# Rotary projection stage: other order of projections, scores one block ahead, sine product written by DVE in four pieces

## The chip, the cores and the metric

The kernel runs on one core of a Trainium2 chip. The metric is the device time of one execution in microseconds (us), the median of a few runs. Engines are named as in the profile: PE is TensorE's matmul, PEld its weight load, DVE is VectorE, ACT is ScalarE, POOL is GpSimd, SP is SyncE, which here issues most of the DMAs.

## The reference, cut to what matters

Sixteen meta tokens and 512 frames (L = 528 tokens of 1024 features) go through two layers. A layer has an attention and pooling half and a gated MLP half:

```
xn = rms_norm(h, attn_norm_g[l]);  q, k, v, u = split(xn @ w_in[l])      # 512, 128, 128, 512 columns
q = apply_rope(rms_norm(q, q_norm_g[l]), cos, sin) * HEAD_DIM ** -0.5     # 8 heads of 64
k = apply_rope(rms_norm(k, k_norm_g[l]), cos, sin)                        # 2 heads of 64
attn = sliding_sink_attention(q, k, v, sinks[l])    # chunks of 64, a window of 2 chunks, plus meta keys
pool = multiscale_pool(u, w_pool[l], pool_scale[l]) # 4 groups of 128 channels, trailing means over 2/4/8/16
h = h + concat(attn, pool) @ w_out[l]
xn = rms_norm(h, ffn_norm_g[l]);  h = h + (gelu(dwconv(xn @ w_gate)) * (xn @ w_up)) @ w_down
```

The rotation of a head is `[x1*c - x2*s, x2*c + x1*s]` with x1, x2 the two halves of 32 features: each half needs the other half's product with the sine.

## The kernel before

Features lie on the partitions and tokens on the free axis, so a tile is 128x528. Each fp32 operand is split into a high and a low part (`x_hi`, `x_lo`, `w_hi`, `w_lo`; line 443 makes three products of them), and ACT (line 337) and DVE (line 348) make the two parts of each weight unit of 256 columns, which SP loads into `raw`. One projection of 128 columns is 8 feature tiles x 3 products x 2 token halves, 48 matmuls.

Five engine programs are written out by hand and run in parallel, with semaphores between them; nothing reorders them. An engine does its instructions in the written order, so one that waits holds up everything behind it. PE's order in a layer's first half is: projections k, v, the column mean of the squares for the norm (L453), q0, the transposes of v (`v_T`, L513), the mean of k's squares, q1, q2, the q means of the first two heads' tiles (`q_means`, L499), q3, u3 and the first 5 of 48 rows of the remaining u groups, the second q means, and then the loop over the 9 blocks of queries: `scores` (L561), some rows of the side projection (`project_side`, u2, u1, u0, which go through a slice of PSUM called slot 4), `heads` (L588, L595), `probs_T` (L573, L576), and the four maps of the pooled groups.

The rotation of the four q tiles and of k works through DVE, ACT and POOL. DVE scales the projected tile (L1078, `head` or `k_dup`), multiplies it by the sine table into a buffer `sine`, which is the tile of v_T (L1097, for k L1094), ACT copies `sine` to `rot_s` with the 32-partition quarters swapped (`shift`, L844, four copies), POOL multiplies by the cosine (`rot_c`, L729, L724) and adds the two into `q_rot` (L733 for the meta tokens, L734 for the rest); k's sum is made by DVE in four pieces (L1131). There is one `rot_c`, one `rot_s` and one `sine`, so a tile's rotation waits for the one before.

```
def shift(n):
    act.wait_ge(sine_ready, l * 5 + (n + 1))
    ...
    for to, fr in ((0, 32), (32, 0), (64, 96), (96, 64)):
        ins = nc.scalar.activation(rot_s[to:to + 32], sine[fr:fr + 32], ACT.Copy)
    ins.then_inc(rots_ready, 1)
```

In the block loop, step b has PE's scores of block b, DVE's row maxima of b (L1170 to L1175), ACT's exponentials of b (L919), and DVE's division of block b-1 (L1181 to L1189).

Of the kernel before, what the change touches and what calls it, by code (L numbers as in the profile page):

```python
# [28 lines left out]
EPS = 1e-6  # L29
# [17 lines left out]
U_KV, U_Q, U_U23, U_U01, U_POOL, U_OUT = 0, 1, 3, 4, 5, 6  # L47
# [16 lines left out]
class Psum:  # L64
# [7 lines left out]
    def __init__(self):  # L72
        self.at, self.uses = {}, [0, 0, 0, 0, 0]
        order = [("k", 2), ("v", 3), ("attn_norm", 0), ("q0", 1), ("v_T", 0), ("k_sq", 3), ("q1", 2),
                 ("q2", 1), ("qn0", 0), ("q3", 3), ("u3", 2), ("qn1", 0)]
        for b in range(NB):
            order += [(f"scores{b}", 1 - b % 2)] + {5: [("pool3", 1)], 8: [("pool2", 0), ("pool1", 0)]}.get(b, [])
        order += [("pool0", 1)] + [(f"{kind}{b}", s) for b in range(NB) for kind, s in (("probs_T", 2), ("heads", 3))]
        order += [(f"u{g}{half}", 4) for g in (2, 1, 0) for half in "ab"]
# [21 lines left out]
def build_trunk(nc, x, meta_tokens, attn_norm_g, w_in, q_norm_g, k_norm_g, sinks, w_pool, pool_scale,  # L101
# [5 lines left out]
    with ExitStack() as ctx:  # L107
# [26 lines left out]
        eps = sb(ctx, "eps", [P, 1])  # L134


        with ExitStack() as sc:
# [18 lines left out]
            sine = v_T[:]  # L156
            rot_c = sb(sc, "rot_c", [P, L])
            rot_s = sb(sc, "rot_s", [P, L])
# [20 lines left out]
        with ExitStack() as sc:  # L179
            x_in = sb(sc, "x_in", [P, SEQ // P, D_MODEL])  # L180
            meta_in = sb(sc, "meta_in", [N_META, D_MODEL])
            par_in = sb(sc, "par_in", [NPAR, DEPTH, P])
            sink_in = sb(sc, "sink_in", [P, DEPTH, 2, 2])
            y_out = sb(sc, "y_out", [P, SEQ // P, D_MODEL])

# [7 lines left out]
        def tok(ap):  # L193
# [12 lines left out]
        eps_ready = sem("eps_ready")  # L206
        h_copied = sem("h_copied")
# [12 lines left out]
        sine_ready = sem("sine_ready")  # L220
        rots_ready = sem("rots_ready")
# [19 lines left out]
        MIX_ORDER = ["heads0", "heads1", "heads2", "pool3", "heads3", "heads4", "heads5", "pool2", "heads6",  # L241
                     "pool1", "heads7", "heads8", "pool0"]
# [11 lines left out]
        GROUPS = (3, 2, 1, 0)  # L254
# [3 lines left out]
        POOLED_AT, POOL_HI_AT, POOL_LO_AT, MAP_AT = (1, 4, 6, 9), (2, 5, 7, 9), (3, 6, 9, 9), (5, 8, 9, 10)  # L258
# [16 lines left out]
        def rotated_before(l, n):  # L275

            name = ROTATED[n - 1]
# [28 lines left out]
        def last_user_done(l, unit, i=0):  # L306
# [17 lines left out]
            else:  # L324
                name = ("v", "q1", "q3", "u2b", "u0b", "pool0")[old]
# [40 lines left out]
        def _(sp):  # L366
            sp.dma_start(cst[:, 0:C_CNT], const[:, 0:C_CNT]).then_inc(ident_loaded, 16)
            kv_cols = blocks(w_in[0])[:, :, ATTN_WIDTH:ATTN_WIDTH + UC]
            for t in range(SEQ // P):
                if t == 2:  # L370
                    sp.dma_start(raw[0][:, :, 0:P], kv_cols[:, :, 0:P]).then_inc(kraw_loaded, 16)
                sp.dma_start(x_in[:, t], x[0, t * P:(t + 1) * P, :]).then_inc(x_loaded[t], 16)
            for a in (0, 4):
                sp.dma_start(raw[0][:, a:a + 4, P:UC], kv_cols[:, a:a + 4, P:UC]).then_inc(raw_loaded[0], 16)
# [45 lines left out]
        def _(pe):  # L420
# [61 lines left out]

            eight = [(k, k) for k in range(KT)]
            for l in range(DEPTH):
                def project(name, unit, ready=None):
                    c = int(name in ("v", "u3", "q1", "q3"))
# [3 lines left out]
                    elif c == 0 or name == "u3" or (l == 0 and name == "v"):  # L490
# [868 lines left out]
```

## Time and profile before

| what | value |
|---|---|
| median of 3 runs | 1100.2 us (1099.22 to 1102.31) |
| the profiled execution, its own time | 1100.07 us |
| its span (first to last instruction) | 1098.3 us |
| PE busy | 1064.2 us, 97% of the span |
| DVE busy, ACT busy, POOL busy | 522.4, 471.3, 123.3 us |
| mean granted TensorE clock | 0.988 of full speed |

A busy share is a mean over stages. The MLP halves take most of the span and the attention halves lie at 17 to 127 us and at 561 to 667 us; what a change of the attention half is worth is read there, from what PE waits for.

### The profile page before, as it was taken

How to read it: one execution, taken by the hardware profiler on the slowest of the kernel's cores; microseconds unless marked ns; L12 is line 12 of the kernel's file. 1: busy time of each engine (PE TensorE's matmuls, PEld its weight loads, DVE VectorE, ACT ScalarE, POOL GpSimd, SP SyncE). 2: the span in 40 equal slices, each digit the busy share in tenths (PEclk: the TensorE clock that was granted, in tenths of full speed). 3: DMA queues.
4: the chain of work that ended last, by engine and by line, in shares of the span. 5: the costliest groups of instructions: out<-in, count | busy, mean ns of one | idle time of the engine just before them, and what ended most of it. 6: DMA issues, size and time to landing. Idle time of an engine off the chain costs nothing.

```text
span 1098.3 us, 18457 instructions
## 1 busy us (share of the span) xinstructions
PE 1064.2 (97%) x7668; PEld 1001.0 (91%) x7668; DVE 522.4 (48%) x690; ACT 471.3 (43%) x662; POOL 123.3 (11%) x121
## 2 busy tenths in 40 slices
PE   6998899999999999999999989999999999999997
PEld 6897799999999999999999978999988999888886
DVE  5667645545445545232336576455455544532221
ACT  5775435444444444122237664364344543421110
POOL 1262000111000111000003510000001100000000
PEclk9989999999999999999999899999999999999999
DMA  6311222322322322323321112223223232233212
GB/s 201 103 49 40 77 77 77 103 89 77 114 76 76 105 86 70 103 78 105 104 78 49 39 40 97 96 77 108 84 76 114 77 111 80 76 106 106 72 61 77
DMA packets 93518, 94.30 MB, mean 86 GB/s; under 512 B 3392, under 2 KB 91800, under 8 KB 93480
## 3 DMA queue, kind: packets, MB, share of 16 engines
q1 hardware_dynamic: 92768, 93.01, 26.4%
q0 software_dynamic: 400, 0.58, 0.2%
q8 instruction: 27, 0.44, 0.2%
q10 hardware_dynamic: 312, 0.18, 0.1%
q14 instruction: 11, 0.09, 0.0%
HBM read 91.65 MB, written 2.10 MB: 85 GB/s over the span
## 4 chain that ended last, share of the span: by engine, by line
PE 82%; ACT 8%; DVE 7%; issue 1%; DMA 1%; SPq 0%; POOL 0%; DVEq 0%; ACTq 0%; POOLq 0%
PE slot L443 80%; ACT probs L919 3%; ACT w_hi L337 1%; DVE nmax L1170 1%; DMA x_in<-in_x 1%; ACT rot_s L844 1%; DVE ms_work L1121 1%; DVE probs L1189 1%; DVE w_lo L348 1%; DVE mix_lo L1205 0%; ACT x_hi L778 0%; DVE den L1181 0%; DVE sumsq L1046 0%; DVE sink_arg L1175 0%; ACT pool_hi L852 0%
## 5 line engine op out<-in xcount | busy, mean ns | idle before, releaser
L443 PE MATMUL slot<-x_hi,w_hi 128*128 128x264 f32 (+1 forms) x1552 | 364.1, 302 | 5.4 <-DVE x_lo L1033 2.7
L443 PE MATMUL slot<-x_lo,w_hi 128*128 128x264 f32 (+1 forms) x1552 | 361.0, 300 | 0.0
L443 PE MATMUL slot<-x_hi,w_lo 128*128 128x264 f32 (+1 forms) x1552 | 360.2, 299 | 0.0
L348 DVE TENSOR_TENSOR w_lo<-raw,w_hi 128x2048 fp32r<-128x2048 f32 (+2 forms) x87 | 194.6, 2237 | 247.6 <-ACT w_hi L337 247.6
L337 ACT ACTIVATE w_hi<-raw 128x2048 fp32r<-128x2048 f32 (+3 forms) x89 | 160.8, 1806 | 260.8 <-PE slot L443 259.5
L443 PEld LDWEIGHTS slot<-x_hi,w_hi 128*128 128x128 f32 x1552 | 254.4, 190 | 17.4 <-DVE u_sb L1152 3.9
L443 PEld LDWEIGHTS slot<-x_lo,w_hi 128*128 128x128 f32 x1552 | 253.0, 190 | 7.3
L443 PEld LDWEIGHTS slot<-x_hi,w_lo 128*128 128x128 f32 x1552 | 252.6, 191 | 7.4
L443 PE MATMUL slot<-m_hi,w_lo 128*128 128x264 f32 (+1 forms) x528 | 140.7, 321 | 0.0
L443 PE MATMUL slot<-m_hi,w_hi 128*128 128x264 f32 (+1 forms) x528 | 140.4, 320 | 0.0
L443 PE MATMUL slot<-m_lo,w_hi 128*128 128x264 f32 (+1 forms) x528 | 140.3, 320 | 0.0
L764 POOL TENSOR_TENSOR up<-up,conv 128x528 f32<-128x528 f32 (+1 forms) x44 | 57.6, 1310 | 577.1 <-ACT conv L989 542.3
L984 ACT ACTIVATE conv<-gate,cpar 128x528 f32<-128x528 f32 (+1 forms) x44 | 36.2, 823 | 151.4 <-DVE gate L1078 151.4
L443 PEld LDWEIGHTS slot<-m_lo,w_hi 128*128 128x128 f32 x528 | 87.6, 188 | 7.9
L443 PEld LDWEIGHTS slot<-m_hi,w_lo 128*128 128x128 f32 x528 | 87.4, 188 | 7.6
L443 PEld LDWEIGHTS slot<-m_hi,w_hi 128*128 128x128 f32 x528 | 87.6, 188 | 7.4
L1078 DVE TENSOR_TENSOR gate<-slot,rinv 128x528 f32<-128x528 f32 x44 | 31.1, 708 | 113.6 <-PE slot L443 113.3
L989 ACT ACTIVATE conv<-conv 128x528 f32<-128x528 f32 (+1 forms) x44 | 28.1, 640 | 73.7 <-DVE conv L1277 73.7
L443 PE MATMUL slot<-mix_hi,w_lo 128*128 128x264 f32 x256 | 52.1, 285 | 0.0
L443 PE MATMUL slot<-mix_hi,w_hi 128*128 128x264 f32 x256 | 52.1, 285 | 0.0
L443 PE MATMUL slot<-mix_lo,w_hi 128*128 128x264 f32 x256 | 51.9, 284 | 0.0
L1248 DVE TENSOR_TENSOR h<-slot,h 128x528 f32<-128x528 f32 x24 | 16.9, 706 | 54.5 <-PE slot L443 54.0
(142 smaller groups left out, 931.3 us busy)
## 6 DMA issues: line engine op xcount, KB each, us to landing
raw<-in_w_gate SPq DMA_DIRECT2D x44, 512.0 KB, 4.6
raw<-in_w_up SPq DMA_DIRECT2D x44, 512.0 KB, 4.4
raw<-in_w_down SPq DMA_DIRECT2D x32, 512.0 KB, 4.3
raw<-in_w_in SPq DMA_DIRECT2D x19, 512.0 KB, 4.9
raw<-in_w_out SPq DMA_DIRECT2D x16, 512.0 KB, 4.5
raw<-in_w_down SPq DMA_DIRECT2D x16, 384.0 KB, 3.6
x_in<-in_x SPq DMA_DIRECT2D x4, 512.0 KB, 7.7
out<-y_out SPq DMA_DIRECT2D x8, 256.0 KB, 3.0
```

The source lines that it names most:

```text
L337: ins = nc.scalar.activation(w_hi[s][:, a:b], raw[s][:, a:b], ACT.Copy)
L348: ins = nc.vector.tensor_tensor(w_lo[s][:, a:b], raw[s][:, a:b], w_hi[s][:, a:b].bitcast(f32), ALU.subtract)
L443: ins = nc.tensor.matmul(out_part, w[ws][:, r, cols], a[:, k, tokens], start=first and n == 0 and w is w_hi and a is a_hi, stop=end and w ...
L764: nc.gpsimd.tensor_tensor(up[c][:, t0:], up[c][:, t0:], conv[c][:, t0:], ALU.mult)\
L844: ins = nc.scalar.activation(rot_s[to:to + 32], sine[fr:fr + 32], ACT.Copy)
L919: ins = nc.scalar.activation(probs[:, y, t, 0:nk], slot[s][:, t // 2, col], ACT.Exp, bias=nm[:, y, t:t + 1], scale=q_scale[:, b, t // 2, t ...
L984: nc.scalar.activation(conv[c][:, t0:], gate[c][:, 2 + t0:], ACT.Identity, bias=cpar[:, 3, c:c + 1], scale=cpar[:, 2, c:c + 1]).then_inc(t ...
L989: nc.scalar.activation(conv[c][:, t0:], conv[c][:, t0:], ACT.Gelu).then_inc(gelu_ready, 1)
L1078: nc.vector.tensor_tensor(tok(dst), halves(s), tok(rinv[:]), ALU.mult).then_inc(evac[s], 1)
L1121: rot.link(nc.vector.reciprocal(ms_work[:], ms_work[:]))
L1170: ch.link(nc.vector.tensor_reduce(nmax[:, y].rearrange("p (a t) -> p a t", a=2), view, op=ALU.max, axis=AX.X, negate=True))
L1248: nc.vector.tensor_tensor(tok(h[:, k]), halves(s), tok(h[:, k]), ALU.add).then_inc(evac[s], 1)
```

## The change

Six things change together.

1. **Sine product.** DVE multiplies quarter by quarter and writes each product of 32 partitions straight to the swapped quarter of `rot_s`; ACT's `shift`, the buffer `sine` and its semaphore are gone. There are now two `rot_c` and two `rot_s` (the second is `run_a`), so a tile waits for the tile two before it.
2. **Order of projections.** PE does k, the norm's mean, q0, k's mean of squares, q1, q2, q means, q3, u3, q means, the scores of block 0, and only then v, with v's transposes in step 1. The side projection's 48 rows all lie in steps 1 to 7. The weight units are cut otherwise (k with the last q tile, the last u group with the first q tile, v with u0).
3. **Look-ahead.** Step b issues the scores and the row maxima of block b+1.
4. **First pool map** in two halves through the side slice of PSUM (`first_map`).
5. **First norm.** In layer 0 the mean square of a token comes from squares of the input rows on ACT (with an accumulated sum), a square root, a reciprocal on DVE and five small matmuls; the eight squares and seven additions of the tiles are gone there.
6. **Splits.** DVE's split of unit 2 moves from the layer's start to behind the sine product of q1, the split of unit 4 behind the first row maxima.

```diff
+            rot_c = [sb(sc, f"rot_c{n}", [P, L])[:] for n in range(2)]
+            rot_s = [sb(sc, "rot_s", [P, L])[:], run_a[:, PAD:]]
...
-                def shift(n):
-                    act.wait_ge(sine_ready, l * 5 + (n + 1))
-                    if n > 0:
-                        act.wait_ge(*rotated_before(l, n))
-                    for to, fr in ((0, 32), (32, 0), (64, 96), (96, 64)):
-                        ins = nc.scalar.activation(rot_s[to:to + 32], sine[fr:fr + 32], ACT.Copy)
-                    ins.then_inc(rots_ready, 1)
...
                 def sine_part(n):
                     name = ROTATED[n]
-                    if n > 0:
-                        dve.wait_ge(rots_ready, l * 5 + n)
+                    if n >= 2:
+                        dve.wait_ge(*rotated(l, n - 2))
+                    src, table = k_dup[:, 0], sin
...
-                    nc.vector.tensor_tensor(sine, head[:, int(name[1]) % 2], q_sin, ALU.mult).then_inc(sine_ready, 1)
+                        src, table = head[:, int(name[1]) % 2], q_sin
+                    for to, fr in ((0, 32), (32, 0), (64, 96), (96, 64)):
+                        ins = nc.vector.tensor_tensor(rot_s[n % 2][to:to + 32], src[fr:fr + 32], table[fr:fr + 32],
+                                                      ALU.mult)
+                    ins.then_inc(rots_ready[n % 2], 1)
...
                 sine_part(1)
                 q_tile(1)
+                sine_part(2)
+                split_lo(dve, l, 2)
                 dve.wait_ge(rotc_ready, l + 1)
...
-                sine_part(2)
+                q_tile(2)
+                sine_part(3)
                 split_lo(dve, l, 3)
-                for j in (2, 3):
-                    q_tile(j)
-                    sine_part(j + 1)
-                split_lo(dve, l, 4)
+                q_tile(3)
+                sine_part(4)
                 scaled("u3", u_sb[:, 0, PAD:])
...
+                scores(0)
+                project("v", U_VU0)
                 for step in range(NB + 2):
-                    if step < NB:
-                        scores(step)
+                    if step == 1:
+                        v_transposed()
...
                     project_side(first, min(cut, end))
+                    if step + 1 < NB:
+                        scores(step + 1)
...
-        SIDE_ENDS = [5, 8, 14, 20, 26, 32, 38, 44, 48, 48, 48, 48, 48]
+        SIDE_ENDS = [0, 0, 7, 14, 21, 28, 34, 41, 48, 48, 48, 48, 48]
```

On DVE, in the projection stage of layer 0, this stood before (`v_T<-head,sq` and `v_T<-k_dup,cst` are the sine products, `w_lo` the split of a weight unit):

```order
L1078 TENSOR_TENSOR k_dup<-slot2,rinv 128x528
L1078 TENSOR_TENSOR v_T<-slot3,rinv 128x528
L1078 TENSOR_TENSOR head<-slot1,rinv 128x528
L1097 TENSOR_TENSOR v_T<-head,sq 128x528
L1121 RECIPROCAL ms_work<-ms_work 128x528
L1122 SCALAR_TENSOR_TENSOR k_dup<-k_dup,par_all,ms_work 128x528
L1094 TENSOR_TENSOR v_T<-k_dup,cst 128x528
L1078 TENSOR_TENSOR head<-slot2,rinv 128x528
L1131 TENSOR_TENSOR k_dup<-rot_c,rot_s 64x528 x4
L1097 TENSOR_TENSOR v_T<-head,sq 128x528
L348 TENSOR_TENSOR w_lo1<-raw1,w_hi1 128x2048
```

and this stands there now, from the same instruction on:

```order
L1126 TENSOR_TENSOR k_dup<-slot2,rinv 128x528
L1126 TENSOR_TENSOR head<-slot3,rinv 128x528
L1149 TENSOR_TENSOR rot_s<-head,sq 32x528 x4
L1173 RECIPROCAL ms_work<-ms_work 128x528
L1174 SCALAR_TENSOR_TENSOR k_dup<-k_dup,par_all,ms_work 128x528
L1149 TENSOR_TENSOR run_a<-k_dup,cst 32x528 x4
L1126 TENSOR_TENSOR head<-slot1,rinv 128x528
L1149 TENSOR_TENSOR rot_s<-head,sq 32x528 x4
L357 TENSOR_TENSOR w_lo0<-raw0,w_hi0 128x2048
L1185 TENSOR_TENSOR k_dup<-rot_c1,run_a 64x528 x4
L1126 TENSOR_TENSOR head<-slot0,rinv 128x528
L1149 TENSOR_TENSOR run_a<-head,sq 32x528 x4
```

Each sine product is four instructions instead of one, v's scaling has left this stage, q1's sine product and the split of unit 2 stand ahead of k's sum.

On PE, behind q2, before (the q means, then q3, which waits only for its PSUM slot):

```order
L443 MATMUL slot<-x_lo,w_hi 128x264 x2
L443 MATMUL slot<-x_hi,w_lo 128x264 x2
L499 MATMUL slot<-cst,head_sq 128x2 [waits headsq_ready,evac0]
L499 MATMUL slot<-cst,head_sq 128x2 x8
L443 MATMUL slot<-x_hi,w_hi 128x264 [waits evac3]
```

and now:

```order
L458 MATMUL slot<-x_lo,w_hi 128x264 x2
L458 MATMUL slot<-x_hi,w_lo 128x264 x2
L513 MATMUL slot<-cst,head_sq 128x2 [waits headsq_ready,evac2]
L513 MATMUL slot<-cst,head_sq 128x2 x8
L458 MATMUL slot<-x_hi,w_hi 128x264 [waits lo_split0,evac3]
```

q3 now waits for DVE's split of unit 2 (`lo_split0`) as well.

On PE at the first scores, before (behind them come rows of the side projection, which wait for nothing):

```order
L499 MATMUL slot<-cst,head_sq 128x2 [waits headsq_ready,evac0]
L499 MATMUL slot<-cst,head_sq 128x2 x8
L561 MATMUL slot<-k_dup,q_rot 128x16 [waits q_ready,k_ready,evac1]
L561 MATMUL slot<-k_dup,q_rot 128x16 x3
L443 MATMUL slot<-x_hi,w_hi 128x264
```

and now (behind them comes the whole of v):

```order
L513 MATMUL slot<-cst,head_sq 128x2 [waits headsq_ready,evac2]
L513 MATMUL slot<-cst,head_sq 128x2 x8
L593 MATMUL slot<-k_dup,q_rot 128x16 [waits q_ready,k_ready,evac0]
L593 MATMUL slot<-k_dup,q_rot 128x16 x3
L458 MATMUL slot<-x_hi,w_hi 128x264 [waits lo_split1,evac3]
```

The first scores wait for the same rotation as before, but v's 48 matmuls, its transposes and the 5 side rows now stand behind this wait instead of ahead of it.

## Rows read from the trace of the kernel before

**Rows 1.** Page, part 1: busy us (share of the span) and instructions

```profile
PE 1064.2 (97%) x7668; PEld 1001.0 (91%) x7668; DVE 522.4 (48%) x690; ACT 471.3 (43%) x662; POOL 123.3 (11%) x121
```

**Rows 2.** Waits of PE: us in total, times, longest us

```profile
PE slot L588 <- DVE mix_lo L1205: 6.5, 8, 1.2
...
PE slot L443 <- DVE u_sb L1152: 2.7, 5, 0.7
...
PE slot L443 <- ACT probs L919: 2.6, 4, 0.9
...
PE slot L499 <- ACT head_sq L828: 1.8, 2, 0.9
...
PE slot L573 <- DVE probs L1189: 1.6, 2, 0.8
...
PE slot L561 <- POOL q_rot L734: 0.9, 1, 0.9
```

**Rows 3.** Windows of the two block loops: us, busy (x) per engine, PEclk, DMA

```profile
72.70:127.10 54.40, 47.26 (x367) 40.27 (x368) 38.59 (x107) 31.22 (x110) 12.01 (x14) 0.91 0.08 27
...
614.30:668.50 54.20, 47.71 (x382) 40.89 (x382) 39.56 (x109) 33.63 (x113) 11.44 (x14) 0.94 0.08 24
```

**Rows 4.** Chain that ended last: start us, us, what

```profile
180.73 392.46 PE slot L443 x3216
```

**Rows 5.** Timeline of PE: start us, us, tile, count [idle before <-releaser]

```profile
72.80 1.04 PE L561 MATMUL slot<-k_dup,q_rot 64*128 64x16 f32 x8 [0.92 <-POOL q_rot L734]
...
580.60 0.96 PE L513 MATMUL slot<-cst,v_T 128*128 128x128 f32 x7 [0.64 <-DVE v_T L1078]
...
595.21 2.14 PE L499 MATMUL slot<-cst,head_sq 128*128 128x2 f32 x18 [0.89 <-ACT head_sq L828]
...
614.35 0.62 PE L561 MATMUL slot<-k_dup,q_rot 64*128 64x16 f32 x8
```

**Rows 6.** Timeline of DVE, first layer's start and second layer's projections

```profile
38.12 0.71 DVE L1078 TENSOR_TENSOR k_dup<-slot,rinv 128x528 f32<-128x528 f32 x1 [1.61 <-ACT rinv L818]
...
575.16 2.29 DVE L348 TENSOR_TENSOR w_lo<-raw,w_hi 128x2048 fp32r<-128x2048 f32 x1 [7.54 <-ACT w_hi L337]
...
579.13 0.71 DVE L1078 TENSOR_TENSOR k_dup<-slot,rinv 128x528 f32<-128x528 f32 x1 [1.68 <-ACT rinv L818]
...
579.75 0.70 DVE L1078 TENSOR_TENSOR v_T<-slot,rinv 128x528 f32<-128x528 f32 x1
...
585.62 3.45 DVE L1121 RECIPROCAL ms_work<-ms_work 128x528 f32<-128x528 f32 x1 [1.25 <-ACT ms_work L885]
...
589.11 0.80 DVE L1122 SCALAR_TENSOR_TENSOR k_dup<-k_dup,par_all,ms_work 128x528 f32<-128x528 f32 x1
...
594.37 2.85 DVE L1131 TENSOR_TENSOR k_dup<-rot_c,rot_s 64x528 f32<-64x528 f32 x4 [2.12 <-ACT rot_s L844]
...
597.88 3.41 DVE L348 TENSOR_TENSOR w_lo<-raw,w_hi 128x2048 fp32r<-128x2048 f32 x1
...
607.90 2.37 DVE L348 TENSOR_TENSOR w_lo<-raw,w_hi 128x2048 fp32r<-128x2048 f32 x1 [0.94 <-ACT w_hi L337]
```

**Rows 7.** Timeline of POOL, second layer's rotation

```profile
597.30 1.83 POOL L729 TENSOR_TENSOR rot_c<-head,sq 128x528 f32<-128x528 f32 x1 [4.48 <-DVE k_dup L1131]
...
608.20 3.25 POOL L729 TENSOR_TENSOR rot_c<-head,sq 128x528 f32<-128x528 f32 x1
...
612.14 0.32 POOL L733 TENSOR_TENSOR q_rot<-rot_c,rot_s 128x64 f32<-128x64 f32 x1 [0.69 <-ACT rot_s L844]
...
612.42 1.26 POOL L734 TENSOR_TENSOR q_rot<-rot_c,rot_s 128x512 f32<-128x512 f32 x1
```

**Rows 8.** Timeline of ACT, second layer

```profile
573.21 1.91 ACT L337 ACTIVATE w_hi<-raw 128x2048 fp32r<-128x2048 f32 x1 [7.92 <-PE slot L443]
...
581.05 0.72 ACT L868 ACTIVATE sq<-cst,par_all 128x528 f32<-128x528 f32 x1
...
586.28 2.61 ACT L844 ACTIVATE rot_s<-v_T 32x528 f32<-32x528 f32 x4
```

More of the change, by code:

```diff
@@ new lines, in _, with v_transposed @@
+                project("u3", U_Q0U3)
+                q_means(1)
+                def v_transposed():
+                    s = open_slot("v_T", l)
+                    pe.wait_ge(evac[ps.slot("v")], ps.before("v", l) + 1)
+                    flat = slot[s][:].rearrange("p a t -> p (a t)")
+                    for w in range(NWIN):
+                        t0 = N_META + w * CHUNK
+                        nc.tensor.transpose(flat[:, w * P:(w + 1) * P], v_T[:, t0:t0 + P], ident)
+                    nc.tensor.transpose(flat[0:N_META, NWIN * P:(NWIN + 1) * P], v_T[:, 0:N_META], ident)\
+                      .then_inc(filled[s], 1)
@@ L537, in project_side, with first_map @@
                             ins.then_inc(filled[4], 1)
+                def first_map(half):
+                    g = GROUPS[0]
+                    name = f"pool{g}{'ab'[half]}"
+                    open_slot(name, l)
+                    if half == 0:
+                        pe.wait_ge(lo_split[U_POOL % 2], slot_turn(l, U_POOL) + 2)
+                        pe.wait_ge(plo_ready, l * 4 + 1)
+                    dense(None, U_POOL % 2, (g % 2) * P, [(g // 2, 0)], pool_hi, pool_lo, part=half)\
+                      .then_inc(filled[4], 1)
                 def pool_map(n):
@@ L623, in _ @@
                         probs_T(step - 1)
+                    if step == MAP_AT[0]:
+                        first_map(1)
                     project_side(cut, end)
@@ L626, in _ @@
                         pool_map(3)
-                rows = [(k, k) for k in (7, 6, 5, 0, 1, 2, 3, 4)]
+                rows = [(k, k) for k in (7, 4, 6, 0, 1, 2, 3, 5)]
                 def mixed(k):
@@ L800, in _ @@
             act.wait_ge(raw_loaded[0], 32)
-            nc.scalar.activation(w_hi[0][:, :, P:UC], raw[0][:, :, P:UC], ACT.Copy).then_inc(hi_split[0], 1)
+            nc.scalar.activation(w_hi[0][:, :, 0:P], raw[0][:, :, 0:P], ACT.Copy).then_inc(hi_split[0], 1)
+            s = ps.slot("attn_norm")
+            act.wait_ge(filled[s], ps.before("attn_norm", 0) + 1)
+            nc.scalar.activation(rinv[:, 0:N_META + 3 * P], slot[s][:, 0, 0:N_META + 3 * P], ACT.Copy)
+            nc.scalar.activation(rinv[:, N_META + 3 * P:], slot[s][:, 1, 0:P], ACT.Copy).then_inc(evac[s], 1)
             split_hi(act, 0, 1)
-            for k in range(KT):
-                square(0, 0, k)
-            act.wait_ge(eps_ready, 1)
             act.wait_ge(prep_ready, 1)
@@ L942, in _ @@
                 for step in range(NB + 3):
+                    if step == 1:
+                        v_windows()
                     if step >= 3 and step != NB:
@@ L951, in _ @@
                         pooled_hi(3)
-                    for n in (0, 1, 2):
+                    for n in (1, 2):
                         if step == MAP_AT[n]:
@@ L959, in _ @@
                         exps(step)
+                    if step == MAP_AT[0]:
+                        for half in range(2):
+                            first_map_hi(half)
                     if step in POOL_HI_AT[0:3]:
@@ L1207, in heads_lo @@
                       .then_inc(evac[hd], 1)
+                row_maxima(0)
+                split_lo(dve, l, 4)
                 for step in range(NB + 3):
+                    if step == 0:
+                        scaled("v", v_T[:])
                     if 3 <= step < NB + 2:
@@ L1236, in _ @@
                         split_lo(dve, l, U_POOL)
+                    if step == MAP_AT[0]:
+                        for half in range(2):
+                            first_map_lo(half)
                 pool_map_lo(3)
```

276 lines of the change are left out of this document (148 added, 128 removed).

## The prediction

> **What bounds the kernel now.** I read the page's busy time first: PE is busy for 1064.2 of 1098.3 us [rows 1], so only PE's idle time and the time it runs at the lower clock can be won or lost; the matmuls themselves are nearly the same ones in the changed kernel. Then PE's list of waits [rows 2]. The six rows sum to 16.0 us in both layers. Four belong to the block loop: the heads wait for `mix_lo` (6.5), side rows wait for `u_sb` (2.7), the exponentials (2.6) and the division (1.6) hold up the rest, 13.4 us in all or 6.7 a layer. Two belong to the projections: the q means wait for squares (1.8) and the first scores for `q_rot` (0.9). The windows of the two loops [rows 3] show 54.40 and 54.20 us with PE busy 47.26 and 47.71, and a granted clock of 0.91 and 0.94 there; a clock of 0.91 means that 18% of that stretch, about 9.8 us, was at 1.2 GHz. Then the chain that ended last: 3216 matmuls of one line in 392.46 us [rows 4], 0.122 us each, so a projection of 48 costs 5.86 us and a side row (3 matmuls) 0.37 us. Last, the timelines of the projection stage, where three engines work on the rotation [rows 5 to 8]. There the reader is to see that DVE and POOL get in each other's way.
>
> **DVE against POOL.** A split that takes 2.29 us alone took 3.41 us at 597.88 while POOL's product ran from 597.30 to 599.13; 597.88 + 3.41 = 601.29, which is 599.13 plus 2.16. The other way round, POOL's product at 608.20 took 3.25 us while a split ran from 607.90 to 610.27; it ended 1.18 us behind the split's end [rows 6, 7]. So one waits out the whole of the other. A POOL product is 1.18 us net and the last addition 0.32 + 1.26 us [rows 7]. DVE instructions with one input from PSUM do not meet this, so I charge it only to those that read two SBUF tensors. The Trainium skill says the same (SBUF — State Buffer, § Who interferes with whom): a VectorE instruction with two SBUF inputs and a GpSimd instruction that reads SBUF exclude each other for a whole instruction. By that rule the change is worse than its instruction counts say, as every new piece reads two SBUF tensors; the rows give the same sum.
>
> **What goes.** ACT loses five times 2.61 us a layer [rows 8]. ACT is not what PE waits for at the end of the stage, the whole rotation is; so this pays only by the latency in the chain. v (5.86), its transposes (0.96, about 0.9 of PE [rows 5]) and 5 side rows (5 x 0.37 = 1.83) move from ahead of the first scores to behind them: 8.6 us of PE work that no longer covers the rotation.
>
> **What comes.** A sine product is four DVE pieces. No row shows a 32-partition DVE piece; the nearest is k's sum, four 64-partition pieces in 2.85 us, 0.71 each [rows 6]. The lower bound is the step of 0.62 us between two full tiles (579.13 to 579.75) [rows 6], 2.5 us a product. I take 2.87 with the gap to the next, since the pieces have the same form. The Trainium skill (VectorE: DVE Perf Modes, § Two Vector instructions with no wait between them) says that an instruction which starts in another group of 32 partitions than the last is held until all earlier ones end; by it the pieces stand at the dearer row, by the plain 0.62 step the sum would be 2 us a layer less.
>
> **DVE's chain in a layer**, from the start of k's scaling (T = 0) to the first scores. The tables are ready at T + 2.64 (581.05 + 0.72 - 579.13) [rows 6, 8]. The first sine product then takes 2.87, and POOL's product (1.2 with its gap) goes between its pieces: 6.7. Reciprocal 3.45: 10.2, with q0's sum on POOL beside it. k's scaling 0.80: 11.0. k's sine 2.87 + 1.2: 15.1. q1 scaled 0.6: 15.7. q1's sine 4.07: 19.8. Split of unit 2, 2.25: 22.0. k's sum 2.87, between whose pieces POOL puts q1's addition, 0.3 + 1.25: 26.4. q2 0.65 and its sine 4.07: 31.2. Split of unit 3: 33.4. q3 0.7: 34.1. q3's sine 2.87, with POOL's product 1.2 and the rest of q2's addition 0.9: 39.1. POOL's last addition 1.55 and latencies 0.3: T + 41.0. Of this POOL's turns are 5 x 1.2 + 0.3 + 1.25 + 0.9 = 8.4 us. Before, the same stretch was 72.80 - 38.12 = 34.7 us in layer 0 and 614.35 - 579.13 = 35.2 in layer 1 [rows 5, 6].
>
> **When it starts.** Layer 1: v (5.86) is no longer ahead of the norm's mean, and ACT's split of 1.91 us at 573.21 no longer ahead of its root [rows 8]: T = 579.13 - 5.86 - 2.2 = 571.1. q0 is filled later here, at 574.2, so the first sine product starts 1.4 us later than the tables alone allow: scores at 571.1 + 1.4 + 41.0 = 613.5. Adding the 8.6 us of moved PE work gives 622.1 to set against 614.35: **7.7 us later**. Layer 0: k's 5.9 us, five small matmuls, ACT's copy, the split of unit 1 (1.9 on ACT and 2.29 on DVE) come one behind another from 18 us on, T = 30.7, and scores at 71.7; plus 8.6 is 80.3 against 72.80: **7.5 us later**. On PE this shows as three new stalls a layer: before the q means (the squares of q1 come at T + 16.6, q2 is done by T + 14 to 15.6), before q3 for the split of unit 2 (about 3.5 us), and before the first scores (about 4 us). Part of q3 and u3 may then run at 1.2 GHz, which costs nothing as long as they end before q3's turn on DVE.
>
> **The block loop.** The look-ahead lets ACT start a block's exponentials without waiting for the division before; of 6.7 us of waits a layer I expect to lose most in the middle. New ones come: v's transposes and side rows behind DVE's v (about 0.8), the first u half (1.1), the two halves of the first map, which go one after the other through ACT, DVE and one PSUM slice (1.9), and the tail, where the exponentials of block 8 still stand behind ACT's copies of step 8 (3.3): 7.1. That is -6.7 + 7.1, so I take nothing; bounds from -5 (all middle waits and the tail go) to +2 a layer. The first norm's squares on ACT delay the first x_hi by about 0.5 us, inside the layer 0 sum.
>
> **Sum.** 7.7 + 7.5 + 0 = 15.2 us. From the profiled execution's 1100.07 (its span plus 1.8) that is 1115; the median of the runs, 1100.2, says the same.
>
> **The rivals.**
> 1. POOL's turns fall into DVE's gaps. If POOL's instructions run while DVE waits or works from PSUM, the 8.4 us a layer drop out: scores at 63.3 and 605.1, with 8.6 added 0.9 us and 0.6 us earlier than before, and the loop's gain of up to 5 a layer comes through: 1094 to 1099, middle 1095. Against it: in the chain above DVE has no gap from T + 2.6 on, and 597.30 and 608.20 show POOL colliding with a DVE that was less full. It decides the sign when the chain from k's scaling to the scores stays under about 33 us. Chance 0.13.
> 2. The chain is as long as I say, but the loop gives back its whole 6.7 us of waits and the low clock of [rows 3] too, about 3 us a layer: 15.2 - 2 x 7.5, 1100. Against it: v's transposes and the split map add waits. Chance 0.08.
> 3. The stalls bring long stretches at 1.2 GHz on q3, u3 and v, and the loop starts so. v alone at 1.2 GHz costs 5.86 more a layer; the loop already loses about 3 to 5 a layer to that level [rows 3], so this is a further 3 to 5 a layer: 1122 to 1125. The Trainium skill (TensorE: Matmul & The Clock Gate) makes the lower clock follow idle time. Chance 0.17.
> 4. My sum, with its bounds (pieces at 0.62: -4; loop +-4): 1108 to 1121. Chance 0.62.
>
> **Numbers.** A measurement of this kernel can tell about 0.3%, 3.3 us. Cases 3 and 4 are slower, case 2 is half the same, half slower or faster: slower 0.81, same 0.07, faster 0.12. The range runs from 1101 (a part of case 2) to 1122.
>
> **What would show it.** In the changed profile: sine pieces of 0.7 us with one of about 1.9 in most groups of four, next to POOL products; a PE wait for the split of unit 2 of 3 to 4 us and for `q_rot` of about 4 us in each layer; the first scores 41 us behind k's scaling; ACT's copies gone with no gain; fewer waits for `mix_lo` and `probs`. I am wrong if the first scores come at T + 35 or less, if the pieces cost well under 0.6 us, or if the loop shrinks by more than 5 us beside the moved work.

## The result, and the profile after

The change took 1125.08 us, median of 4 runs (1122.99 to 1125.57), against 1099.95 us for the kernel before (4 runs, 1099.22 to 1102.31): 1.0213 of its time, interval 1.0193 to 1.0232. The direction was forecast, the size was not: 25 us slower instead of 15, and above the range.

First the page of the changed kernel, part 1 (busy us, share of the span, instructions), which answers to [rows 1].

```profile
PE 1081.8 (96%) x7674; PEld 1016.5 (90%) x7674; DVE 550.0 (49%) x717; ACT 443.9 (39%) x625; POOL 131.2 (12%) x120
```

PE is busy 17.6 us longer with nearly the same matmuls (7674 instructions, before 7668), so much of the loss is matmuls that ran slower. Then PE's list of waits in the changed kernel (us in total, times, longest us), which answers to [rows 2].

```profile
PE slot L513 <- ACT head_sq L878: 4.5, 2, 2.2
...
PE slot L593 <- POOL q_rot L768: 3.6, 2, 1.8
...
PE slot L620 <- DVE mix_lo L1265: 3.5, 6, 0.7
...
PE slot L458 <- DVE mix_lo L1211: 3.3, 4, 1.1
...
PE slot L458 <- DVE w_lo L357: 3.2, 2, 1.6
...
PE slot L605 <- DVE probs L1249: 2.6, 2, 1.3
```

The three projection waits of the forecast are there (squares for the q means, split `w_lo`, `q_rot`), 4.5, 3.2 and 3.6 us for two layers. The wait for the exponentials is gone; that of line 620 for `mix_lo` (line 588 before) fell from 6.5 to 3.5. In their place stand the first map (`mix_lo` at line 458, 3.3), a wait of the third map for `pool_lo` (2.0, not shown) and a longer wait for the division (2.6 against 1.6).

Now the projection stage of layer 0: the timeline of DVE (start us, us, line, output and inputs, count).

```profile
31.62 0.71 DVE L1126 TENSOR_TENSOR k_dup<-slot,rinv 128x528 f32<-128x528 f32 x1 [0.22 <-DVE par_all L1111]
...
34.37 3.90 DVE L1149 TENSOR_TENSOR rot_s<-head,sq 32x528 f32<-32x528 f32 x4 [1.17 <-ACT sq L915]
...
42.66 3.99 DVE L1149 TENSOR_TENSOR run_a<-k_dup,cst 32x528 f32<-32x528 f32 x4
...
47.49 3.86 DVE L1149 TENSOR_TENSOR rot_s<-head,sq 32x528 f32<-32x528 f32 x4
...
53.59 3.96 DVE L1185 TENSOR_TENSOR k_dup<-rot_c,run_a 64x528 f32<-64x528 f32 x4
...
58.39 3.88 DVE L1149 TENSOR_TENSOR run_a<-head,sq 32x528 f32<-32x528 f32 x4
...
65.33 4.47 DVE L1149 TENSOR_TENSOR rot_s<-head,sq 32x528 f32<-32x528 f32 x4
```

And of POOL at the same time.

```profile
34.52 1.75 POOL L762 TENSOR_TENSOR rot_c<-head,sq 128x528 f32<-128x528 f32 x1 [2.23 <-ACT sq L915]
...
47.52 1.84 POOL L762 TENSOR_TENSOR rot_c<-head,sq 128x528 f32<-128x528 f32 x1 [3.57 <-issue]
...
51.49 2.36 POOL L767 TENSOR_TENSOR q_rot<-rot_c,rot_s 128x64 f32<-128x64 f32 x1 [2.13 <-DVE rot_s L1149]
...
70.22 1.27 POOL L768 TENSOR_TENSOR q_rot<-rot_c,rot_s 128x512 f32<-128x512 f32 x1
```

Each group of four sine pieces takes 3.9 to 4.0 us, the last 4.5, as forecast with POOL's product in every one of them: alone they would be some 2.85. In the first group three pieces take 0.70 us and one takes 1.75. At 51.49 an addition of 64 columns, which takes 0.33 us elsewhere, takes 2.36, because it waits out DVE's split from 51.38 to 53.67. Last, the timeline of PE at the three stalls of the stage, and the first scores of both layers.

```profile
48.34 3.92 PE L513 MATMUL slot<-cst,head_sq 128*128 128x2 f32 x18 [2.24 <-ACT head_sq L878]
...
53.82 0.78 PE L458 MATMUL slot<-x_hi,w_hi 128*128 128x264 f32 x2 [1.56 <-DVE w_lo L357]
...
71.64 0.62 PE L593 MATMUL slot<-k_dup,q_rot 64*128 64x16 f32 x8 [1.78 <-POOL q_rot L768]
...
624.54 0.62 PE L593 MATMUL slot<-k_dup,q_rot 64*128 64x16 f32 x8 [1.77 <-POOL q_rot L768]
```

From k's scaling (31.62) to the first scores (71.64) are 40.0 us, in layer 1 (583.24 to 624.54) 41.3. The q means, 2.14 us before [rows 5], take 3.92: the granted clock was 0.51 there, so PE was at 1.2 GHz.

The rest of the loss is in the block loop. The first scores are at 71.64 and 624.54, against 72.80 and 614.35 [rows 5]; the out projection starts at 137.65 and 690.54, against 127.03 and 666.79. I cut the loop where the second pool map starts (121.63 and 674.52, before 114.15 and 655.27). A row of windows gives the stretch and its length, the busy time of PE, PEld, DVE, ACT and POOL, and then the granted clock and the DMA's share. The windows of the changed kernel are, in this order: layer 0 up to that cut, layer 0 behind it, layer 1 up to it; and last, for each layer, the stretch at 1.2 GHz around the loop's end.

```profile
71.64:121.63 49.99, 46.69 (x374) 41.73 (x374) 30.58 (x89) 25.79 (x97) 11.28 (x11) 0.93 0.13 43
121.63:137.65 16.02, 11.89 (x68) 9.32 (x66) 11.88 (x23) 9.10 (x21) 2.82 (x3) 0.66 0.01 2
624.54:674.52 49.98, 46.68 (x374) 41.73 (x374) 30.58 (x89) 25.81 (x97) 11.26 (x11) 0.93 0.13 43
126.90:140.60 13.70, 11.84 (x55) 10.04 (x56) 8.54 (x15) 8.44 (x18) 0.00 (x0) 0.50 0.24 79
679.90:693.60 13.70, 11.87 (x56) 10.06 (x57) 8.54 (x15) 8.33 (x17) 0.00 (x0) 0.50 0.24 79
```

The kernel before, in the same cut (layer 0 up to it, layer 0 behind it):

```profile
72.80:114.15 41.35, 37.66 (x303) 32.66 (x303) 27.89 (x83) 22.31 (x89) 11.91 (x14) 0.92 0.10 33
114.15:127.03 12.88, 9.53 (x64) 7.51 (x65) 10.71 (x24) 8.80 (x22) 0.00 (x0) 0.87 0.02 4
```

| stretch | before | after | lost |
|---|---|---|---|
| up to the first scores of layer 0 (8.6 us of PE work moved behind them) | 72.80 | 71.64 + 8.6 | 7.4 |
| up to the first scores of layer 1, without the 12.1 lost in layer 0 | 614.35 | 624.54 + 8.6 - 12.1 | 6.7 |
| first scores to the second pool map, layer 0 | 41.35 + 8.6 | 49.99 | 0.0 |
| the same, layer 1 | 40.92 + 8.6 | 49.98 | 0.5 |
| second pool map to the out projection, layer 0 | 12.88 | 16.02 | 3.1 |
| the same, layer 1 | 11.52 | 16.02 | 4.5 |
| out projection's first matmuls at 1.2 GHz, both layers | 0 | 3.0 | 3.0 |

The 3.0 of the last row is half of what remained at 1.2 GHz behind the loop's end (140.6 - 137.65 and 693.6 - 690.54). The rows sum to 25.2 us, of 25.5 between the two profiled executions (1125.57 and 1100.07). Up to the cut the loop is neutral. Behind it the granted clock is 0.66 in the changed kernel, 0.87 before, and PE's busy time grew from 9.5 to 11.9 us for the same work. Below, the stretch from the scores of the last block to the out projection is called the tail (18.46 us in both layers).

### The profile page after: what moved, and what is told of

Its sections match the earlier page's. It is cut to its first block, busy times and chain, and to the rows that moved or that the text cites. A ratio compares the mean times of both kernels' runs of the same rounds, so it can differ in the third digit from the quotient of the medians.

```text
span 1123.8 us, 18438 instructions
## 1 busy us (share of the span) xinstructions
PE 1081.8 (96%) x7674; PEld 1016.5 (90%) x7674; DVE 550.0 (49%) x717; ACT 443.9 (39%) x625; POOL 131.2 (12%) x120
## 4 chain that ended last, share of the span: by engine, by line
PE 87%; DVE 8%; ACT 1%; issue 1%; DMA 1%; POOL 0%; ACTq 0%; DVEq 0%; POOLq 0%
PE slot L458 84%; DVE rot_s L1149 2%; DVE run_a L1149 1%; PE slot L593 1%; DVE k_dup L1185 1%; DMA par_in<-in_conv_w 1%; DVE w_lo L357 1%; DVE ms_work L1173 1%; PE slot L620 1%; PE slot L627 1%; DVE head L1126 0%; DVE nmax L1230 0%; PE slot L721 0%; PE slot L608 0%; ACT probs L963 0%
## 5 line engine op out<-in xcount | busy, mean ns | idle before, releaser
L357 DVE TENSOR_TENSOR w_lo<-raw,w_hi 128x2048 fp32r<-128x2048 f32 (+2 forms) x87 | 192.1, 2208 | 242.0 <-ACT w_hi L346 241.9
```

The lines of the kernel that those rows point to most:

```text
L357: ins = nc.vector.tensor_tensor(w_lo[s][:, a:b], raw[s][:, a:b], w_hi[s][:, a:b].bitcast(f32), ALU.subtract)
```

## The experiments

The theory after the result had two parts. Theory 1: the pieces, with POOL's turns between them, make the projection chain 10 us a layer longer than it needs to be. Theory 2: the loss behind the cut belongs to the changed order, not to the pieces: the exponentials of the last block stand late on ACT, and PE, with little to do there, falls to 1.2 GHz. The rivals: the pieces' number alone makes the chain long; the changed order itself costs most; the lower clock is only a by-product hidden behind ACT's and DVE's chain. The kernel before, run beside the first four, took 1101.25 us; beside the next four 1100.45; beside the last two 1101.54.

**e1_copies: the change, with the swap back on ACT.** DVE makes the product in one instruction, alternately into two free buffers; ACT copies the four quarters.

```diff
-for to, fr in ((0, 32), (32, 0), (64, 96), (96, 64)):
-    ins = nc.vector.tensor_tensor(rot_s[n % 2][to:to + 32], src[fr:fr + 32], table[fr:fr + 32], ALU.mult)
-ins.then_inc(rots_ready[n % 2], 1)
+nc.vector.tensor_tensor(sine[n % 2], src, table, ALU.mult).then_inc(sine_ready, 1)   # sine = [v_T, run_b]
...
+def shift(n):      # on ACT
+    for to, fr in ((0, 32), (32, 0), (64, 96), (96, 64)):
+        ins = nc.scalar.activation(rot_s[n % 2][to:to + 32], sine[n % 2][fr:fr + 32], ACT.Copy)
```

> The changed kernel with the sine product back in one DVE instruction per tile and the swap on ACT (two sine buffers). Theory 1 (the lengthened DVE and POOL chain of the rotation costs 14 of the 25 us): first scores about 31 us behind k's scaling instead of 40.0, time 1105 to 1109. Rival (the new order and the look-ahead cost it, whoever swaps): the pieces hardly matter, time stays at 1118 or more.

Measured: 1101.55 us (10 runs, 1099.97 to 1105.33), 1.0005 of the kernel before (0.9990 to 1.0021). The pieces cost 23.5 us in this order, and all the rest of the change is in sum worth nothing: in layer 0 the first scores come 2.4 us earlier than before (61.80 + 8.6 against 72.80) and the loop is 1.5 us longer. Which of the other five changes gives and which takes was not run. Of the 23.5, 20 are the chain (40.0 and 41.3 us with pieces, 30.0 and 31.3 here); 4.2 are in the loops (66.0 twice against 64.4 and 63.4), which "What stays open" takes up. 1101.55 is below what I expected (1105 to 1109). The timeline of DVE in this kernel:

```profile
31.78 0.71 DVE L1141 TENSOR_TENSOR k_dup<-slot,rinv 128x528 f32<-128x528 f32 x1 [0.22 <-DVE par_all L1126]
...
34.53 0.71 DVE L1163 TENSOR_TENSOR v_T<-head,sq 128x528 f32<-128x528 f32 x1 [1.15 <-ACT sq L925]
...
39.68 1.61 DVE L1163 TENSOR_TENSOR run_b<-k_dup,cst 128x528 f32<-128x528 f32 x1
...
42.02 1.03 DVE L1163 TENSOR_TENSOR v_T<-head,sq 128x528 f32<-128x528 f32 x1
...
51.05 0.71 DVE L1163 TENSOR_TENSOR run_b<-head,sq 128x528 f32<-128x528 f32 x1
```

And of PE, the two groups of q means and the first scores:

```profile
46.08 2.06 PE L515 MATMUL slot<-cst,head_sq 128*128 128x2 f32 x18
...
59.81 2.06 PE L515 MATMUL slot<-cst,head_sq 128*128 128x2 f32 x18
...
61.80 0.62 PE L595 MATMUL slot<-k_dup,q_rot 64*128 64x16 f32 x8
```

No row there has a wait in brackets: but for 0.76 us at the norm's mean (33.39), where the change has 0.77, the projections run through, the q means take 2.06, and the scores come 30.0 us behind k's scaling. So PE's own work is the bound of this stage. POOL's last addition ends at 61.60, only 0.2 us ahead of the scores, so what the pieces add to the chain is seen nearly whole. The stretch behind the last scores is as long as in the change: 107.90 to 126.16 is 18.3 us, in layer 1 18.9, against 18.5 (119.19 to 137.65). The tail's loss is not the pieces'.

**e2_before_pieces: the kernel before, with only the pieces.** The orders stay, ACT's copies go.

```diff
-nc.vector.tensor_tensor(sine, head[:, int(name[1]) % 2], q_sin, ALU.mult).then_inc(sine_ready, 1)
+for to, fr in ((0, 32), (32, 0), (64, 96), (96, 64)):
+    ins = nc.vector.tensor_tensor(rot_s[to:to + 32], src[fr:fr + 32], table[fr:fr + 32], ALU.mult)
+ins.then_inc(rots_ready, 1)
```

> The kernel before with nothing changed but the sine product in four DVE pieces and no copies on ACT. Theory 1: the rotation chain becomes about 4 us longer than PE's cover in each layer, 1106 to 1110. Rival (v, its transposes and the side rows still cover it): 1099 to 1102.

Measured: 1109.42 us (1108.70 to 1110.54), 1.0071 (1.0043 to 1.0098), as expected. PE's list of waits in this kernel has most of the price in one row (0.9 us before [rows 2]):

```profile
PE slot L561 <- POOL q_rot L734: 5.7, 2, 3.7
```

From k's scaling (37.79) to the first scores (77.17) are 39.4 us, against 34.7 before; in layer 1 (582.28 to 621.68) 39.4 against 35.2. So even in the order of before, where ACT's copies are in the chain and v's projection covers a part of it, replacing them by pieces costs 8 us.

**e3_exps8: the change, with the last exponentials early.** ACT does those of block 8 first in step 8, ahead of a split, a map copy, the copy of head tile 6 and the probabilities of block 7. The timeline of the change has, on DVE, the last step of their input, and on ACT what stands ahead of them.

```profile
121.18 0.16 DVE L1235 TENSOR_TENSOR sink_arg<-nm,sink_all 128x4 f32<-128x4 f32 x1
...
122.40 1.05 ACT L346 ACTIVATE w_hi<-raw 128x1024 fp32r<-128x1024 f32 x1
...
126.25 0.60 ACT L974 ACTIVATE probs_win<-slot 128x512 f32<-128x512 f32 x1 [1.64 <-PE slot L608]
...
126.75 0.20 ACT L960 ACTIVATE sink_exp<-sink_arg 128x4 f32<-128x4 f32 x1
```

The input is there at 121.3 us, they start at 126.75.

```diff
+if step == NB - 1:
+    exps(step)
 if step == 8:
     split_hi(act, l, U_OUT, half=0)
...
-if step < NB:
+if step < NB - 1:
     exps(step)
```

> The changed kernel with ACT's exponentials of block 8 ahead of its split, map copy and head copies of step 8. Theory 2 (the loop's end is a chain in which they stand behind work that waits for PE, and PE then runs at 1.2 GHz): the stretch from the last scores to the output projection, 18.5 us, becomes 3 to 5 us shorter in each layer, time 1115 to 1119. Rival (the end is bound by the maps and heads themselves): 1123 to 1126.

Measured: 1116.53 us (1114.99 to 1119.08), 1.0131 (1.0098 to 1.0164): 8.6 us won. Not all of it is the edit's: 1.5 us a layer lie between the first and the last scores (46.06 and 45.97 us instead of 47.55 and 47.54), where the edit does nothing. The windows from the last scores to the out projection, first of this kernel's layers 0 and 1, then of the change's:

```profile
118.86:133.69 14.83, 10.64 (x90) 8.19 (x89) 12.86 (x27) 9.26 (x22) 2.82 (x3) 1.00 0.00 1
665.31:682.95 17.64, 14.26 (x91) 11.39 (x90) 13.32 (x27) 9.37 (x22) 2.82 (x3) 0.69 0.03 2
```

```profile
119.19:137.65 18.46, 14.33 (x91) 11.32 (x90) 13.41 (x27) 9.48 (x22) 2.82 (x3) 0.71 0.01 2
672.08:690.54 18.46, 14.31 (x90) 11.30 (x90) 13.41 (x27) 9.48 (x22) 2.82 (x3) 0.71 0.02 4
```

The profiled execution happened to have one tail at each level. In layer 0 the granted clock is 1.00 and the tail takes 14.83 us; in layer 1, with the same instructions, the clock is 0.69 and it takes 17.64. The same tail on the lower clock is 2.8 us longer, and the out projection then starts low: another 1.4. So a low tail costs 4.2 us a layer. The order alone is seen in layer 1, low in both kernels: 17.64 against 18.46, 0.8 us.

**e4_one_piece: the change, one DVE product without the swap.** The quarters are not exchanged, and ACT has no copies either.

```diff
-for to, fr in ((0, 32), (32, 0), (64, 96), (96, 64)):
-    ins = nc.vector.tensor_tensor(rot_s[n % 2][to:to + 32], src[fr:fr + 32], table[fr:fr + 32], ALU.mult)
-ins.then_inc(rots_ready[n % 2], 1)
+nc.vector.tensor_tensor(rot_s[n % 2], src, table, ALU.mult).then_inc(rots_ready[n % 2], 1)
```

> The changed kernel with the sine product as one 128-partition instruction written without the swap of the quarters (the rotation is then not the reference's): the cost of four pieces against one. Theory 1: DVE's chain is 5 x 2.25 = 11 us a layer shorter, first scores about 29 us behind k's scaling, 1103 to 1107. Rival: POOL's turns or the loop keep the time at 1115 or more.

Measured: 1102.3 us (one run), scores 30.0 us behind k's scaling. It is the time of e1_copies: five copies of 2.61 us a layer on ACT cost nothing that shows. The work that the change saved was free, the work that it put in its place was not.

**e5_memset: the change, POOL's cosine products replaced by writes of a constant.** These read no SBUF.

```diff
-nc.gpsimd.tensor_tensor(rot_c[n % 2], k_dup[:, 0], cos, ALU.mult).then_inc(rotc_ready, 1)
+nc.gpsimd.memset(rot_c[n % 2], 0.5).then_inc(rotc_ready, 1)
...
-steps.link(nc.gpsimd.tensor_tensor(rot_c[n % 2], head[:, j % 2], q_cos, ALU.mult))
+steps.link(nc.gpsimd.memset(rot_c[n % 2], 0.5))
```

> The changed kernel, with POOL's five cosine products a layer replaced by instructions that only write a constant into the same buffers, so they read no SBUF (the rotation is then not the reference's). Theory 1 (my chain's sum: besides the pieces, POOL's turns of 1.2 us each are waited out by DVE): the sine groups of four lose their long piece, the stretch from k's scaling to the first scores shrinks from 40.0 to about 34 us (5 x 1.2 less), and the time falls by up to 12 us, less what other waits (the splits, the squares) take over: 1112 to 1118. Rival (the pieces' number alone makes the chain long, POOL hides in DVE's gaps): the stretch stays at 39 to 41 us and the time at 1122 to 1126.

Measured: 1111.32 us (1110.63 to 1112.15), 1.0103 (1.0085 to 1.0120), just below the 1112 to 1118 that theory 1 gave. The timeline of DVE in this kernel, four of the five groups of pieces, and of POOL's write beside the first:

```profile
34.63 2.84 DVE L1149 TENSOR_TENSOR rot_s<-head,sq 32x528 f32<-32x528 f32 x4 [1.15 <-ACT sq L915]
...
41.86 2.84 DVE L1149 TENSOR_TENSOR run_a<-k_dup,cst 32x528 f32<-32x528 f32 x4
...
45.55 2.84 DVE L1149 TENSOR_TENSOR rot_s<-head,sq 32x528 f32<-32x528 f32 x4
...
61.31 3.42 DVE L1149 TENSOR_TENSOR rot_s<-head,sq 32x528 f32<-32x528 f32 x4
```

```profile
34.74 0.54 POOL L762 MEMSET rot_c<- 128x528 f32 x1 [2.19 <-ACT sq L915]
```

Four of the five groups take 2.84 us, 0.71 a piece (the sum had 2.87 with the gap to the next); the last, 3.42, lies beside the rest of POOL's addition. A constant written by POOL doesn't hold DVE up. The scores come 35.5 us behind k's scaling (31.88 to 67.34), in layer 1 36.0 (575.61 to 611.57), so POOL's five products were 4.5 and 5.3 us of the chain's 40.0 and 41.3, and the pieces' number the rest of what lies above the 30.0 and 31.3 of e1_copies. The other 4 us that this kernel won are in its loops (63.5 and 64.5 us instead of 66.0), at a granted clock of 0.90 and 0.91 instead of 0.87. By the Trainium skill (SBUF — State Buffer, § Who interferes with whom) a DVE instruction with two SBUF inputs contends with a GpSimd instruction that reads SBUF, and not with one that only writes it, over a pair of ports that is locked for a whole instruction; the trace agrees: beside the write a group took 2.84 us, beside a product 1.0 to 1.15 us more.

**e6_copies_exps8: both mends that paid,** the edits of e1_copies and e3_exps8 together.

> The changed kernel with the sine product as one instruction and the swap by ACT's copies (as in the run that measured 1101.55), and the exponentials of the last block ahead of ACT's copies of step 8 (as in the run that gained 8.6 us on the change). Theory (the tail's loss is the place of the last exponentials and is there with and without the pieces): the tail from the last scores to the out projection falls from 18.3 to about 15 us in both layers and the time is 1093 to 1098, below both kernels. Rival (the 8.6 us were bound to the pieces' timing): 1100 to 1103.

Measured: 1096.51 us (12 runs, 1094.48 to 1099.34), 0.9967 (0.9957 to 0.9977). This is faster than both kernels, than the kernel before by 0.3%. The tails take 16.5 us (108.41 to 124.90) and 14.8 (646.65 to 661.48), where e1_copies had 18.3 and 18.9: so the gain wasn't bound to the pieces.

**e7_fill: the change, with matmuls that nobody reads.** 24 a layer, of 264 columns, in the last three steps of the loop, ahead of the instructions that wait there (5 and 5 before the last two `heads`, 6 before the third pool map, 8 before the probabilities of block 7).

```diff
+def fill(count):
+    pe.wait_ge(evac[4], ps.before(side_name(5), l) + 1)
+    for _ in range(count):
+        nc.tensor.matmul(side, x_hi[:, 0, 0:P], x_hi[:, 1, 0:HALF], start=True, stop=True)
...
+if step >= NB:
+    fill(5)
 if step >= 2:
     heads(step - 2)
+if step == NB:
+    fill(6)
...
+if step == NB - 1:
+    fill(8)
 if 1 <= step <= NB:
     probs_T(step - 1)
```

> The changed kernel, with 24 matmuls of 264 columns that nobody reads (0.12 us each, 2.9 us a layer) put on PE in the last three steps of the block loop, ahead of the instructions that wait there; nothing is left out. Theory (what the tail loses beyond its waits is the 1.2 GHz that follows PE's idling there; in a run with one tail at each level it was 2.9 us of the tail and 1.5 us of the out projection): the low stretches of 13.7 us near 127 and 680 us go, the matmuls lie mostly in the waits (1.30, 0.73, 0.97, 0.73), and the time is 1117 to 1121. Rival (the lower clock in the tail is hidden behind ACT's and DVE's chain, or filling doesn't raise it): the time stays at 1123 to 1128, the filler on top.

Measured: 1119.10 us (1118.44 to 1120.17), 1.0174 (1.0156 to 1.0192), 6.0 us less than the change, with more work. The window of this kernel over the stretch that was at 1.2 GHz in the change's layer 0:

```profile
126.90:140.60 13.70, 11.49 (x93) 10.27 (x93) 9.82 (x14) 7.62 (x15) 0.00 (x0) 1.00 0.23 78
```

The granted clock is 1.00 where it was 0.50. The tails take 16.70 and 16.69 us instead of 18.46, and the out projections start at 2.4 GHz, which is another 1.5 us each. So the lower clock is no by-product: it was on the path, and more work for PE in the tail lifted it.

**e8_best: e6_copies_exps8 with the filler.**

> The copies for the swap, the last exponentials early and the 24 filling matmuls together. Theory: the filler gives a further 2 to 6 us on the version without it, if PE is at 1.2 GHz in a tail there: 1088 to 1096. Rival: no low stretch is left to win, and the filler costs its own time, up to 3 us: 1095 to 1100.

Measured: 1094.88 us (6 runs, 1094.28 to 1095.85), 0.9951 (0.9938 to 0.9964). The windows of its two tails:

```profile
109.56:124.57 15.01, 13.66 (x114) 11.20 (x113) 12.94 (x27) 9.33 (x22) 2.81 (x3) 1.00 0.00 1
646.37:661.39 15.02, 13.67 (x115) 11.21 (x114) 12.95 (x27) 9.34 (x22) 2.82 (x3) 1.00 0.00 1
```

15.0 us each at a clock of 1.00. Over e6_copies_exps8 this is 1.6 us, where the theory gave at least 2; its layer 1 had already 14.8 us, so only layer 0's 16.5 could be mended. The two profiled executions are no help with so small a difference: their spans are 1093.4 and 1093.5 us, since the one with the filler lost in layer 0, between the first and the last scores, what it won in the tail (47.54 against 46.03 us). It is the fastest version found, 5.6 us below the kernel before.

**e9_exps8_fill: the change with both mends of the tail, pieces and all.**

> The changed kernel with both mends of the tail: the last block's exponentials early, and the 24 filling matmuls. Theory (the block loop's loss over my forecast is the tail alone, its order of work and its low clock; the projection stage's 14.1 us stay): the loop comes back to its length before, give or take 3 us, and the time is 1110 to 1116. Rival (the two mends win the same microseconds): it stays at the better one's 1116.5, up to 1119.

Measured: 1114.13 us (1113.47 to 1116.08), 1.0118 (1.0090 to 1.0146). The windows of its two block loops, from the first scores to the out projection:

```profile
71.90:132.91 61.01, 56.36 (x461) 49.38 (x461) 42.00 (x110) 35.19 (x118) 14.09 (x14) 0.97 0.11 36
618.61:679.68 61.07, 56.42 (x461) 49.44 (x461) 42.01 (x110) 34.92 (x118) 14.10 (x14) 0.97 0.11 36
```

61.0 and 61.1 us, against 62.8 and 61.0 for the kernel before with the 8.6 us moved in. Of the 5 us that each loop won, 3.4 are the tail (15.0 instead of 18.46) and 1.5 lie between the first and the last scores, where neither mend does anything. The loop is back to its length, and what is left, 12.6 us, is the projection stage's 14.1 less the 1.8 won in layer 0's loop, within 0.3. The forecast of 1115 fits this kernel, not the one that ran.

**e10_before_fill: the kernel before, with the same filler at the same steps.**

> The kernel before with the same 24 filling matmuls at the same three places of its last steps. Theory (its tail has a low stretch of 3.4 us in layer 0 alone, so there is little to win): 1098 to 1103, no difference that can be told. Rival (filling pays in any such tail): 1093 to 1097.

Measured: 1102.61 us (1100.84 to 1105.24), 1.0013 (0.9996 to 1.0029): no difference. In layer 0 the filler took away the low stretch, and the loop took 53.94 us instead of 54.23; in layer 1, where that tail had been at 2.4 GHz anyway, it took 53.48 instead of 52.44. So the filler costs about a microsecond where the clock doesn't fall.

## Why the prediction was right on the chain and wrong on the loop

**What bounds the kernel, DVE against POOL: right.** The chain over DVE and POOL set the first scores. Pieces of 0.71, POOL's product in each group, the whole turns: the timelines after show them one by one, and e5_memset takes POOL's part out and gets 2.84 for a group, where the sum had 2.87. The dearer row was the one to take: four pieces alone took 2.84 us, not the 2.5 of the step of 0.62 between full tiles.

**The chain: right.** Forecast 41.0 us from k's scaling to the first scores, and 42.4 in layer 1 where q0 is filled later; measured 40.0 and 41.3. In layer 0 k's scaling came 0.9 us later than forecast, which makes up for the shorter chain. Forecast lost 7.5 and 7.7 us in the layers, measured 7.4 and 6.7. The stalls on PE were mis-shared: before q3 1.6 us instead of 3.5, before the first scores 1.8 instead of 4, and 2.2 before the q means; the rest of the idle time went into matmuls at 1.2 GHz (q means 3.92 us). The sum stayed, because DVE and POOL, not PE, set the end.

**"ACT loses five times 2.61 us": worth nothing.** e4_one_piece and e1_copies are the same time. The prediction had "this pays only by the latency in the chain", and it did not pay by that either: with the copies in place the stage takes 30.0 us, without them and without pieces 30.0 too, since PE's own work is its bound in both. The one wait of DVE for the copies in the rows before (2.12 us [rows 6]) is not there in e1_copies.

**The block loop: the step that failed.** "That is -6.7 + 7.1, so I take nothing; bounds from -5 to +2 a layer." Measured were +3.1 and +5.0 in the two loops and 1.5 more in each out projection, 11.1 us in all, of which 10.6 behind the cut (the start of the second pool map). The waits themselves were not far off. Up to the cut they are 3.3 us in layer 0, against 3.7 before (new ones: v's transposes 0.3, the first map 2.2, forecast 0.8 + 1.9), and the length is the same. Behind the cut they are 4.0 against 3.3. What the sum left out is the clock: I had weighed 1.2 GHz for q3, u3, v and the start of the loop (the third rival, 1122 to 1125), and not for its tail, where the reordered loop has its last scores a step earlier and PE only short groups between waits. e7_fill puts it at 3.3 us a layer (18.46 - 16.70, and 1.5 in the out projection) and e3_exps8 at 4.2 (one tail at each level, 2.8 + 1.4 us apart), 6.5 to 8.4 of the 10.6. The late exponentials of block 8, which I had named and priced at 3.3, are part of what PE waits for there: starting them first took 1.7 us off a tail at the full clock (16.70 in e7_fill, 15.02 in e9_exps8_fill), and in one layer of two the low clock with it. The third rival, which had a chance of 0.17 and was left out of the range, had the right time by the right mechanism in the wrong place; that the size came out as well is luck, since q3 and the start of v did run at 1.2 GHz without adding to the forecast's loss.

**Sums that don't come out as written.** The six waits sum to 16.1 us, not 16.0. The second rival's 6.7 and 3 us a layer are 9.7, where its sum takes 7.5. The fourth case's -4 and +-4 around 1115 are 1107 to 1119, not 1108 to 1121. The forecast of 1115 rests on none of the three, and the measured time lies outside either way.

**What stays open.** Why the clock falls in the tail of one layer and not of the other with the same instructions (e3_exps8; e6_copies_exps8 had 16.5 and 14.8 us) isn't settled by these runs. The same question stands ahead of the tail. These are the windows from the first to the last scores, with the same instructions of PE in them: the change in layer 0, then e1_copies in layers 0 and 1.

```profile
71.64:119.19 47.55, 44.25 (x349) 39.72 (x349) 29.05 (x83) 25.41 (x96) 11.28 (x11) 0.93 0.14 45
61.80:107.90 46.10, 42.81 (x349) 38.28 (x348) 29.22 (x84) 27.12 (x97) 11.21 (x11) 0.96 0.14 47
602.49:646.97 44.48, 41.19 (x350) 36.66 (x349) 29.18 (x84) 27.14 (x97) 11.19 (x11) 1.00 0.15 49
```

The length follows the granted clock (0.93, 0.96, 1.00), as PE's busy time does. The change falls to 1.2 GHz there a second time, behind the waits of the first map: from 109.50 to 113.00 us its granted clock is 0.55, in layer 1 from 662.50 to 666.50 it is 0.57, where e1_copies is at full speed. So the clock accounts for the 1.6 and 2.6 us by which its loops are longer than those of e1_copies: 1.5 and 3.1 us lie in these windows, and 0.2 and -0.5 in the tails. What makes the clock fall there in one kernel and not in the other isn't shown; neither is it shown whether the change would lose these microseconds in every execution.

## What to carry to other kernels

Before an instruction is taken off an engine, see whether anyone waits for it: ACT's 13 us a layer were free, while 15 more DVE instructions a layer cost 23.5 us over both layers, 20 of them in the chain, since a piece of 32 partitions takes as long as the whole tile and each group also lets POOL in. When a loop is reordered, price its tail apart, with the clock: add up what PE does between the waits there, and if the tail was at 2.4 GHz before, ask whether it still will be. A transfer, a copy or an exponential that stands behind other work in the last step can cost twice, by its own wait and, as in one of two tails here, by the lower clock of what follows; a few idle-time matmuls that nobody reads show within one run how much of a loss is the clock.

## What the runs showed of the hardware

A DVE product of 32 partitions by 528 columns took 0.71 us (2.84 for four), and one of 128 partitions by 528 took 0.71 as well (34.53 in e1_copies). The Trainium skill (VectorE: DVE Perf Modes, § Two Vector instructions with no wait between them) has an instruction that starts in another group of 32 partitions wait for all earlier ones to end; the trace agrees, with 0.71 a piece and not 0.62.

In the change's tails PE waited 0.28, 1.30 and 0.73 us, no longer, and from 126.90 on was at 1.2 GHz, for the 13.70 us of the window; 24 unread matmuls a layer in those waits kept it at 2.4 GHz. I had taken the falling clock for a matter of stalls of 3 to 4 us, as those before q3 and the first scores. The waits alone don't tell it either: in e3_exps8 PE waited 0.29 and 1.29 us in the tail of layer 0 and went on at 2.4 GHz, and 0.30 and 1.30 us in that of layer 1 and then fell to 1.2 GHz, near 672 us.

POOL's write of a constant over 528 columns (0.54 us at 34.74 in e5_memset) ran beside DVE's pieces without lengthening them; its product over the same columns lengthened each group by 1.0 to 1.15 us.
